# Layer 1's sixteen experts: from one product of whole matrices to seven products of quarters

## The reference, cut to what matters

```python
def expert_choice_ffn(h, w_router, w_gate, w_up, w_down):
    cap = CAPACITY_FACTOR * n // N_EXPERTS          # 128 tokens
    aff = softmax(h @ w_router)
    gate, idx = lax.top_k(aff transposed, cap)
    xg = h[bidx, idx]                               # [16, 128, 1024]
    hid = silu(xg @ w_gate) * (xg @ w_up)           # weights [16, 1024, 1024] each
    out = (hid @ w_down) * gate[..., None]
    return zeros_like(h).at[bidx, idx].add(out)
...
x = x + gt2 * rmsnorm(expert_choice_ffn(h, ...), g_post_ffn)
```

## Time and profile before

| | us |
|---|---|
| median of three runs | 3475.31 |
| lowest and highest | 3470.2, 3479.14 |
| the profiled execution | 3467.26 |
| its span | 3465.5 |
| PE busy in the span | 3213.0 (93%) |
| DVE, ACT, POOL busy | 1221.2, 948.7, 493.6 |

### The profile page before, as it was taken

The page is one execution under the profiler, slowest core; times in us unless marked ns, Lnnn a source line. Parts: engine busy times, 40 slices in busy tenths (PEclk is TensorE's granted clock), DMA queues, the critical chain, the costliest instruction groups (busy, mean ns, idle before and its releaser), DMA issues. The chain is left out here.

```text
span 3465.5 us, 52549 instructions
## 1 busy us (share of the span) xinstructions
PE 3213.0 (93%) x20008; PEld 2413.8 (70%) x20008; DVE 1221.2 (35%) x2974; ACT 948.7 (27%) x2231; POOL 493.6 (14%) x639
## 2 busy tenths in 40 slices
PE   5999989989987999999999799898999399999998
PEld 3888856667434788787887565665764288888886
DVE  3312178767554110110101253656775511111113
ACT  3211156756340111111101242244644111111111
POOL 0010235110110101111011210344001000000002
PEclk9999999999987999999999899999999599999999
DMA  6335354052639977777777710101314688888987
GB/s 227 122 112 106 81 192 121 19 129 82 238 120 341 356 269 253 243 260 264 265 256 244 261 68 1 61 26 45 79 39 170 243 309 315 315 315 315 315 315 273
DMA packets 389540, 672.38 MB, mean 194 GB/s; under 512 B 84040, under 2 KB 133064, under 8 KB 383168
## 3 DMA queue, kind: packets, MB, share of 16 engines
q1 hardware_dynamic: 357520, 567.98, 47.6%
q0 software_dynamic: 13616, 47.32, 5.7%
q10 hardware_dynamic: 18256, 55.17, 4.3%
HBM read 585.65 MB, written 90.97 MB: 195 GB/s over the span
## 5 line engine op out<-in xcount | busy, mean ns | idle before, releaser
L2731 PE MATMUL experts_gu_ps<-experts_xT,experts_wg 128*128 128x160 f32 (+1 forms) x4096 | 552.1, 288 | 5.6 <-DVE experts_xT L2605 2.6
L2731 PE MATMUL experts_gu_ps<-experts_xT,experts_wu 128*128 128x160 f32 (+1 forms) x4096 | 549.8, 287 | 0.0
L2731 PEld LDWEIGHTS experts_gu_ps<-experts_xT,experts_wg 128*128 128x128 f32 x4096 | 529.2, 192 | 20.6 <-issue 19.4
L2731 PEld LDWEIGHTS experts_gu_ps<-experts_xT,experts_wu 128*128 128x128 f32 x4096 | 525.3, 191 | 0.0
L2628 DVE TENSOR_TENSOR experts_hid<-experts_sil,experts_gu_ps 128x160 f32<-128x160 f32 (+1 forms) x256 | 77.9, 304 | 921.1 <-ACT experts_sil L2559 917.0
L2559 ACT ACTIVATE experts_sil<-experts_gu_ps 128x160 f32<-128x160 f32 (+1 forms) x256 | 74.2, 290 | 1101.0 <-PE experts_gu_ps L2731 1101.0
L2697 PE MATMUL experts_y_ps<-down_ahead_wd,experts_hid 128*128 128x512 f32 x512 | 228.3, 599 | 0.0
L2697 PE MATMUL experts_y_ps<-experts_wd,experts_hid 128*128 128x512 f32 x512 | 224.0, 595 | 1.2 <-DVE experts_hid L2628 1.2
L2697 PEld LDWEIGHTS experts_y_ps<-experts_wd,experts_hid 128*128 128x128 f32 x512 | 96.0, 190 | 118.1 <-issue 114.8
L2646 DVE TENSOR_SCALAR experts_y<-experts_y_ps,experts_wt 128x512 f32<-128x512 f32 x31 | 23.3, 751 | 436.8 <-PE experts_y_ps L2697 436.8
L2697 PEld LDWEIGHTS experts_y_ps<-down_ahead_wd,experts_hid 128*128 128x128 f32 x512 | 94.6, 190 | 114.4 <-issue 113.7
(11 more groups left out here) (489 smaller groups left out, 4844.1 us busy)
## 6 DMA issues: line engine op xcount, KB each, us to landing
experts_wg<-in_l_w_gate SPq DMA_DIRECT2D x64, 2048.0 KB, 8.4
experts_wu<-in_l_w_up SPq DMA_DIRECT2D x64, 2048.0 KB, 13.9
down_ahead_wd<-in_l_w_down SPq DMA_DIRECT2D x32, 2048.0 KB, 10.9
experts_wd<-in_l_w_down SPq DMA_DIRECT2D x32, 2048.0 KB, 11.7
down_ahead_wd<-in_l_w_mod SPq DMA_DIRECT2D x16, 1024.0 KB, 8.9
proj<-proj_ob ACTq DMA_DIRECT2D x60, 256.0 KB, 2.3
first_w<-in_l_w_in SPq DMA_DIRECT2D x6, 2048.0 KB, 10.6
attn_a_mod_w<-in_l_w_mod ACTq DMA_DIRECT2D x12, 1024.0 KB, 7.0
```

What stands on the lines that cost most here:

```text
L2731: mm = nc.tensor.matmul(GU[f % 2][:, part, 0:N], w[:, h, k, c * P:(c + 1) * P], xT[:, k, :], start=(k == 0), stop=(k == KD - 1))
```

## The change

Layer 1 gets its own function, `last_experts`. The three 1024 x 1024 weight matrices of an expert and the tokens (2 x 64) are cut into quarters, and each product of four quarters is computed from seven products of sums (numbered 1 to 7) instead of eight. Each product is 8 matmuls (16 in the record) with 64 columns of tokens stationary and 256 columns of weights moving, written alternately to partitions 0 to 63 and 64 to 127 of a PSUM bank, that is by PE's two column halves. The sums of weights (128 x 2048 elements each) are computed anew for every expert: POOL computes two for gate, two for up and one for down, DVE computes two for gate, two for up and three for down. DVE also computes four sums of tokens for `xT` and four for `hT`, adds the products' parts from PSUM and the copies that ACT kept (`quarter`), and multiplies gate by up with both operands in SBUF (`hidden`). The hidden rows must now be turned by PE (`turn_hidden`). All eight blocks of `xT` are scaled by ACT. Weights are loaded in two halves of 512 full rows (4 KB per row), each after the product that reads it last. The residual rows are loaded into the place of the gate weights after the last expert's gate product, the sums `moe` into the place of the down sums; POOL gates every other one of them. The two scatters of an expert go to half rows.

Elsewhere: the first 2 MB of `w_in` are loaded inside `project`, and the bias by SP in place of ACT; the softmax factor is turned into the round of the weights and copied along with it; the band attention cuts its keys at 384 and not at 512; the first two blocks of rows for `mix_out` are loaded in the attention stage before it.

```diff
-        sp.dma_start(self.w[:, 0], self.w_rows[:, :, 0:BANK]).then_inc(self.w_sem[0], 16)
...
+                sp.wait_ge(cleared, START + 2)
+                for j in range(GROUPS):
+                    sp.dma_start(bias[strip(j), :], begun.b_mod[j * BANK:(j + 1) * BANK].rearrange("(a n) -> a n", a=1).broadcast_to([2, BANK])).then_inc(bias_in, 16)
+                sp.dma_start(w[:, 0], w_rows[:, :, 0:BANK]).then_inc(w_sem[0], 16)
...
-                act.wait_ge(cleared, START + 2)
-                for j in range(GROUPS):
-                    act.dma_start(bias[strip(j), :], begun.b_mod[j * BANK:(j + 1) * BANK].rearrange("(a n) -> a n", a=1).broadcast_to([2, BANK])).then_inc(bias_in, 16)
...
+    def load_rows(self, sp):
+
+        first = self.from_rows[0] * P
+        for slot, t in enumerate((0, NTX // 2)):
+            sp.dma_start(self.ot[:, slot, :], self.mixed[t * P:(t + 1) * P, first:first + KD // 2 * P]).then_inc(self.w_in, 16)
...
+                        following.load_rows(sp)
...
-                load(0)
-                load(1)
...
+PRODUCTS = ((5, 1, 3, 6, 2, 7, 4),) * 2 + ((1, 2, 5, 6, 3, 7, 4),)
+KEPT = tuple([p for p in order if p in (1, 5, 6, 7)] for order in PRODUCTS)
+QUARTERS = ((0, 1, 3, 6), (0, 0, 2, 1), (1, 1, 7, 5), (1, 0, 4, 7))
...
+                with sp.Fori(0, E - 1) as e:
+                    for i in range(3):
+                        sp.wait_ge(mm_done, multiplied(e, i, 7))
+                        load(i, 0, e + 1)
+                        sp.wait_ge(mm_done, multiplied(e, i, 4))
+                        load(i, 1, e + 1)
+                sp.wait_ge(mm_done, multiplied(E - 1, GATE, 4))
+                following.load_rows(sp, x)
...
+                def first_sums(e, i):
+
+                    for half in range(2):
+                        pool.wait_ge(w_in[i][half], START + e * 16 + 16)
+                    nc.gpsimd.tensor_tensor(sums_of(i, 5), quarter_of(i, 0, 1), quarter_of(i, 0, 0), ALU.subtract).then_inc(pool_sums[i], 1)
+                    nc.gpsimd.tensor_tensor(quarter_of(i, 0, 1), quarter_of(i, 1, 1), quarter_of(i, 0, 1), ALU.subtract).then_inc(pool_sums[i], 1)
+
+                def third_sum(e):
+
+                    for half in range(2):
+                        pool.wait_ge(w_in[DOWN][half], START + e * 16 + 16)
+                    pool.wait_ge(dve_sums[DOWN], START + e * 3 + 1)
+                    nc.gpsimd.tensor_tensor(quarter_of(DOWN, 0, 1), quarter_of(DOWN, 1, 1), quarter_of(DOWN, 0, 1), ALU.subtract).then_inc(pool_sums[DOWN], 1)
+
...
+                pool.wait_ge(choice.chosen, START + 1)
+                gather(0)
+                for i in (GATE, UP):
+                    first_sums(0, i)
+                pool.wait_ge(choice.pairs, START + 1)
+                pool.sem_inc(y_free, 1)
+                with pool.Fori(0, E - 1) as e:
+                    link.turn(e, 2)
+                    gather(e + 1)
+                    nc.gpsimd.tensor_copy(wt[:].unsqueeze(2), choice.weight_pair[:, :, bass.ds(e, 1)]).then_inc(wt_in, 1)
+                    link(nc.gpsimd.tensor_copy(ixs[:].unsqueeze(2), choice.index_pair[:, :, bass.ds(e, 1)]))
+                    third_sum(e)
+                    for i in (GATE, UP):
+                        first_sums(e + 1, i)
+                    scatter(e)
+                    pool.wait_ge(s_done, e * 32 + 32)
+                    pool.sem_inc(y_free, 1)
...
+                def row_sums(to, of, done, base):
+
+                    a11, a12, a21, a22 = (of[:, k * HALF:(k + 1) * HALF, c * HD:(c + 1) * HD] for c in range(2) for k in range(2))
+                    nc.vector.tensor_tensor(to[:, 0], a21, a22, ALU.add).then_inc(done, 1)
+                    nc.vector.tensor_tensor(to[:, 3], a11, a21, ALU.subtract).then_inc(done, 1)
+                    dve.wait_ge(done, base + 1)
+                    nc.vector.tensor_tensor(to[:, 1], to[:, 0], a11, ALU.subtract).then_inc(done, 1)
+                    dve.wait_ge(done, base + 3)
+                    nc.vector.tensor_tensor(to[:, 2], a12, to[:, 1], ALU.subtract).then_inc(done, 1)
+
+                def second_sum(e, i):
+
+                    if i == DOWN:
+                        dve.wait_ge(dve_sums[DOWN], START + e * 3 + 1)
+                    else:
+                        dve.wait_ge(mm_done, multiplied(e, i, 5))
+                    dve.wait_ge(w_in[i][1], START + e * 16 + 16)
+                    nc.vector.tensor_tensor(sums_of(i, 6), quarter_of(i, 1, 1), sums_of(i, 5), ALU.subtract).then_inc(dve_sums[i], 1)
+
+                def fourth_sum(e, i):
+
+                    dve.wait_ge(mm_done, multiplied(e, i, 5 if i == DOWN else 6))
+                    if i == DOWN:
+                        dve.wait_ge(dve_sums[DOWN], START + e * 3 + 2)
+                    nc.vector.tensor_tensor(sums_of(i, 4), quarter_of(i, 1, 0), sums_of(i, 6), ALU.subtract).then_inc(dve_sums[i], 1)
...
+                def hidden(e, q):
+                    c, h = QUARTERS[q][0:2]
+                    dve.wait_ge(dve_out, quarter_at(e, UP, q))
+                    nc.vector.tensor_tensor(hid[:, c, h, :], hid[:, c, h, :], gate[:, c, h, :], ALU.mult).then_inc(hid_done, 1)
+
+                def gates_and_up(e, last=False):
+                    second_sum(e, GATE)
+                    fourth_sum(e, GATE)
+                    for q in range(4):
+                        quarter(e, GATE, q)
+                    second_sum(e, UP)
+                    if not last:
+                        for half in range(2):
+                            dve.wait_ge(w_in[DOWN][half], START + e * 16 + 16)
+                        nc.vector.tensor_tensor(sums_of(DOWN, 5), quarter_of(DOWN, 0, 1), quarter_of(DOWN, 0, 0), ALU.subtract).then_inc(dve_sums[DOWN], 1)
+                    fourth_sum(e, UP)
+                    dve.wait_ge(sil_done, START + e + 1)
+                    dve.wait_ge(ht_done, START + e * 2)
+                    for q in range(4):
+                        quarter(e, UP, q)
+                        hidden(e, q)
...
+                with dve.Fori(0, E - 1) as e:
+                    gates_and_up(e)
+                    dve.wait_ge(hid_out, START + e * 4 + 4)
+                    row_sums(sh, hT, sh_done, START + e * 4)
+                    second_sum(e, DOWN)
+                    dve.wait_ge(y_free, START + e + 1)
+                    fourth_sum(e, DOWN)
+                    dve.wait_ge(wt_in, START + e + 1)
+                    for q in range(2):
+                        quarter(e, DOWN, q)
+                    dve.wait_ge(xa, START + e + 2)
+                    row_sums(sx, xT, sx_done, START + e * 4 + 4)
+                    for q in range(2, 4):
...
+                    for k in range(HALF):
+                        for j in range(2):
+                            mm = nc.tensor.matmul(bank[j * HD:(j + 1) * HD, 0:COLS], by[k], at[:, k, j, :], start=(k == 0 and p in (1, 2, 4, 5)),
+                                                  stop=(k == HALF - 1 and p in (2, 3, 4, 7)), skip_group_check=True)
+                    mm.then_inc(mm_done, 1)
...
+                with pe.Fori(0, E - 1) as e:
+                    for i in (GATE, UP):
+                        for p in PRODUCTS[i]:
+                            multiply(e, i, p)
+                    turn_hidden(e, 0)
+                    turn_rows(e + 1)
+                    turn_hidden(e, 1)
+                    for p in PRODUCTS[DOWN]:
+                        multiply(e, DOWN, p)
```

424 lines of the change are left out of this document (378 added, 46 removed).

## The result

| | before | changed |
|---|---|---|
| median of three runs | 3475.31 us | 3698.97 us |
| lowest and highest | 3470.2, 3479.14 | 3697.39, 3710.53 |
| the profiled execution | 3467.26 | 3698.97 |
| its span | 3465.5 | 3697.3 |
| mean granted clock | 0.965 | 0.927 |

The ratio is 1.065, with a 95% interval of 1.061 to 1.069: slower, where 3655 us (3480 to 3740) was forecast. One of five executions of experiment 5's kernel took 8566.82 us and the other four 3439 to 3445; it was a slow one and isn't in that kernel's ratio.

What follows compares the result with a forecast made beforehand. PE alone was taken to set the 43.36 us expert period, with DVE and POOL blocking each other after the change. 3467.3 + 190 + 13 + 5 - 8 - 12 = 3655 us, range 3480 to 3740.

Steps and rivals of the forecast that it cites:

- small moves: Outside the experts: `mix_out` rows loaded earlier -8 us, bias on SP at the start -12, softmax factor and band cut 0.
- start of layer 1's experts: From choice of tokens to first product: four POOL sums, ACT's scaling and token sums delay PE, +13 us.
- fifteen periods: Layer 1's expert loop: each period 56 us instead of 43.36, 12.6 us more each, +190 us.
- last expert: Old-width down product, gates partly on POOL, residual loaded after the last gate product: +5 us (-5 to +15).
- Products and sums: Per expert: a product 1.75 us, POOL's sum 4.5, DVE's 2.3, short operations 0.425; PE 38.6 us without waits.
- rival C: Expert products: column halves don't run side by side at 64 tokens, period 74 us, +460, about 3920; chance 3 in 100.
- The port: Expert loop: DVE operations with both operands in SBUF and POOL's wait for each other's whole; 43.8 us per expert.
- Rival A: Expert loop: no blocking between DVE and POOL, PE stays at 38.6 us per expert, 3385 us; chance 18 in 100.
- Rival B: Expert loop: port blocks but small operations squeeze between, period near 45 us, 3490 us; chance 17 in 100.
- The walk of one expert: One expert traced through the blocking: 38.6 us plus 17.7 of lateness, period 56; chance 62 in 100.
- the clock: PE pausing 5 to 8 us per expert may pay 3 to 5 us more (+75), at the range's high end.

Runs made afterwards that it cites:

- experiment 5: The kernel before with only the change's small moves, layer 1's experts left as they were: 3444.81 us, ratio 0.9906 to the kernel before.
- experiment 1: The changed kernel with POOL's five weight sums per expert left out but for one column each: 3402.22 us, ratio 0.980 to the kernel before.
- experiment 2: The changed kernel with each of POOL's sums cut into four instructions of 512 elements: 3575.33 us, ratio 1.030 to the kernel before.
- experiment 3: The changed kernel with the hidden multiply reading one operand from PSUM in place of SBUF: 3587.51 us, ratio 1.034 to the kernel before.
- experiment 4: The changed kernel with POOL's five sums per expert moved to DVE, POOL keeping two for the first expert: 3454.18 us, ratio 0.9955 to the kernel before.
- Experiment 9: The changed kernel with PE multiplying the identity 22 times, result unused, in its longest pause: 3675.15 us, ratio 1.058 to the kernel before.
- experiment 6: The changed kernel with the last expert's sums loaded from memory ahead of its residual rows: 3705.69 us, ratio 1.067 to the kernel before.
- experiment 10: The changed kernel with all sums on DVE in PE's order, last expert's loads staged and all its gating on DVE: 3397.26 us, ratio 0.978 to the kernel before.

## Why the prediction was right

The forecast was 3655 us for a profiled execution that took 3699, and the mechanism was the one named. Term by term, from the two traces:

| step | forecast | measured |
|---|---|---|
| small moves (start, mix rows, attentions) | -20 | -24 |
| start of layer 1's experts | +13 | +13.2 |
| fifteen periods | +190 (56 us) | +226.5 (58.6 us) |
| last expert | +5 | +15.9 |
| sum | +188 | +232 |

- **Products and sums.** A product of 16 records takes 1.73 us (1.75), POOL's sum 4.5 (4.5), DVE's 2.29 (2.3), a short operation 0.42 (0.425). PE's own 38.6 us per expert is 38.5 by its terms and 38.65 in experiment 1. The column halves do run side by side, so rival C is out.
- **The port.** Rival A, no blocking, would be 3385. Experiment 1, in which nothing is there to block, gave 3402 with the period of 38.8 (38.6), and experiments 2 and 3 show the blocking by the instruction and by the operand. Rival B, a period near 45 us, fell with the 58.6 and the 4.28 us multiplies: in the loop small operations do get in between two of POOL's sums, one per gap, as the walk had it. The Trainium skill, page "SBUF — State Buffer", section "Summary: rules for kernel authors", says of a VectorE instruction with two SBUF inputs and a GpSimd one that reads SBUF that the second to issue fully blocks until the first finishes, and tells authors to schedule whichever is off the critical path. The trace agrees with the first half in the loop (4.28 us for 0.43). At the stage's start it goes further: an operation stayed blocked past the end of the sum that it met, through two more (below, 9.74 us). On the second half no run here moves POOL's sums within its own program; experiment 4 gave them to DVE, the engine that PE waits for, and gained 245 us.
- **The walk of one expert.** The up product's last part was to be 2.8 us late and was 2.73. After it the walk erred both ways, and that the errors nearly cancel is luck. The next gate weights landed at 3005.89, 26.2 us into the expert and not 24, so one more multiply slipped in ahead of POOL and the turned hidden rows came at 31.2 and 36.6 us in place of 34.6 and 40.6. (The walk's own sentence, one multiply before POOL's sums and one between them, would have given about 30; its 34.6 leaves one to come behind both.) The up weights, though, landed at 38.8 us and not 35.8 (37.1 in the expert before), and POOL's two sums fell on the sums of hidden rows: two short operations took 4.74 and 4.62 us (3018.76 and 3023.53), and PE waited 5.46 us for the second down sum where 1.9 were forecast. The product behind that wait stands at 49.3 us in the walk, 56.3 less four products; in the mean of the fifteen experts it came at 49.8. PE waits 13.0 us per expert in the mean, where the forecast had 17.7 of lateness. With its own 38.6 that leaves 7.0 of the 58.6 us, and these are mostly products and turns of rows at the lower clock.
- **The step that was mis-sized: the clock.** I priced the slower clock at 3 to 5 us per expert in the range and at nothing in the sum. Products behind pauses take up to twice as long, and those behind the longest pause lie open, with no wait after them: 3.47 and 2.60 us in place of 1.73 each in the expert shown, 3.38 and 2.03 in the mean of all, so that the last four products take 8.9 us and not 7.0. 49.8 + 8.9 is the period measured, to rounding. The 1.9 us are 28 of the 36.5 by which fifteen periods came out above the sum. Experiment 9 shows the slow products to be due to the pause, and 1.6 us as what filling it is worth. That the slow products behind the shorter pauses only shorten the waits after them is argued; no run fills those pauses.
- **The start.** Index ready to first product took 22.9 us, 9.7 before: +13.2. The token sums didn't pass between POOL's sums, as was forecast. The first was queued at 2732.67 and ended 0.29 us behind the last of POOL's, at 2742.41; the next three took 0.41 or 0.42. That one gets in between in the loop and not here is open. Experiment 4, in which POOL does two sums ahead of the choice and none behind it, has its first product at 2734.30 in place of 2744.64.

```profile
2732.67 9.74 DVE L3051 TENSOR_TENSOR experts_sx<-experts_xT 128x256 f32<-128x256 f32 x1 [9.48 <-ACT experts_xT L2993]
```

```profile
2728.73 4.50 POOL L2928 TENSOR_TENSOR experts_wg<-experts_wg 128x2048 f32<-128x2048 f32 x1
2733.18 4.49 POOL L2927 TENSOR_TENSOR experts_tu<-experts_wu 128x2048 f32<-128x2048 f32 x1
2737.64 4.48 POOL L2928 TENSOR_TENSOR experts_wu<-experts_wu 128x2048 f32<-128x2048 f32 x1
```

- **The last expert.** The forecast was 5, at most 15. I gave PE's 25 us as the cover of the residual's load. But the residual is issued 12.3 us into the expert and the sums behind it, from 16.4 on; the first of these lands at 30.1, and the first square, 14.4 us after the first product in the kernel before, waits for it. Nor did I see that squares and gates had moved behind the hidden rows in ACT's and DVE's programs, which keeps the square at 26.6 us even when the sums are there (experiment 6). DVE's eight gated sums then go at the old pace (21.6 us from the first to the last, 21.1 before), so that the +15.9 comes from their late start, 34.8 us after the first product and not 17.5. In experiment 10 the last expert takes 67.2 us, 5.8 of the 15.9 less; that the order of ACT's and DVE's programs brings the rest wasn't tried.
- **The small moves.** Stage by stage they are 9.5 us at the start (the first projection's first product at 36.19 against 44.98, behind a wait of 2.92 for its weights, and its second at 40.96 against 50.50), about 6.4 in the two attentions and 8 in the two `mix_out`. The attentions, put at nothing give or take 2, gave three times that; the start gave 9.5 and not 12. The two errors leave the sum 4 us short.

```profile
36.19 3.78 PE L554 MATMUL proj_x_ps<-first_w,first_shared 128*128 128x256 f32 x8 [2.92 <-DMA first_w<-in_l_w_in]
```

## What to carry to other kernels

Before work goes to an idle GpSimd, add up what the two engines ask of SBUF together and look at which short VectorE operations on the path of the bottleneck read two operands in SBUF: each may wait for a whole GpSimd instruction, and at the start of this stage one waited for more than two. If so, do the work on VectorE, where a sum took 2.29 us and not 4.5, in the order in which it is wanted; or cut GpSimd's instructions; or let VectorE's operand stay in PSUM. A sum over a walk of one period is worth its trouble, but a bottleneck that starts to pause must be priced at its lower clock in the sum itself, not in the range.

## What the runs showed of the hardware

- An operation of 0.42 us with both operands in SBUF (the hidden multiply) took up to 4.59 us beside GpSimd's sums of 4.5 us, and up to 1.35 beside pieces of them; with one operand in PSUM it took 0.42 or 0.43 in all 64 cases, although its other operand and its output lie in SBUF.
- When both engines have a row of such operations, they take turns in the loop: four VectorE operations of 0.42 us took 1.56, 1.49, 1.49 and 1.37 us. At the stage's start they don't: one took 9.74 us and ended behind the last of three GpSimd sums, and in experiment 2 one took 11.47 us beside the pieces.
- The other way round, a GpSimd sum of 4.54 us took 4.78 when it started 0.37 us before the end of a VectorE sum with both operands in SBUF, and up to 6.58 beside a whole one (experiment 3).
- Two DMA groups on one queue: 2 MB issued ahead of 4 MB landed 9.0 us after issue in the median; the same 2 MB issued behind the 4 MB took 15.3.
- Behind a pause of 5.46 us PE ran a product of 16 records in 3.47 us and the next in 2.60, against 1.73, at granted clocks of 0.50 and 0.66; with matmuls in the pause, 1.77 and 1.72.
